# Layer 2 projections from the unnormalised residual, retention scores by row halves, and regrouped memory waits in a fused transformer kernel

## The reference, cut to what matters

```
mem_n = rmsnorm(mem, mem_norm_g)
for i in range(2):
    h = rmsnorm(x, norm_g[i])                  # x * rsqrt(mean(x*x)+eps) * g
    proj = h @ w_in                            # 1024 -> q, k, v, q_mem, z
    main = fox_attention(...) if i == 0 else retention(...)
    memo = mem_cross_attention(q_mem, mem_n, w_mem_kv[i])
    o = concat([main, memo]) * silu(z)         # 12 main heads, 4 memory heads
    x = x + o @ w_out[i]

retention, 12 heads, key width 64, value width 128:
    q, k = rotary(q), rotary(k) * 64 ** -0.5
    scores = (q @ k.T) * decay(head, lag)
    out = scores @ v                           # in chunks, with a carried state
    out = out * rsqrt(mean(out*out)+eps)
```

## Time and profile before

| | |
|---|---|
| median of 3 runs | 1745.95 us |
| profiled execution, device time | 1745.99 us |
| its span, first to last instruction | 1744.2 us |
| PE busy | 1668.8 us, 96% |
| DVE, ACT, POOL busy | 778.2, 661.2, 677.4 us |
| mean granted TensorE clock | 0.982 |
| share of PE in the chain that ended last | 85% |

### The profile page before, as it was taken

One profiled execution on the slowest core, in us unless ns is written; L12 is line 12 of the kernel. 1 busy time (PEld: TensorE's weight loads), 2 busy tenths in 40 slices (PEclk: granted clock), 3 DMA queues, 4 the chain that ended last, 5 costly groups with the idle time before them and its releaser, 6 DMA issues.

```text
span 1744.2 us, 19924 instructions
## 1 busy us (share of the span) xinstructions
PE 1668.8 (96%) x8216; PEld 1364.2 (78%) x8216; DVE 778.2 (45%) x1117; ACT 661.2 (38%) x962; POOL 677.4 (39%) x320
## 2 busy tenths in 40 slices
PE   8899999999999899999999999989989899999997
PEld 7788788788878687888887758678878688888885
DVE  6338987666664333343442645752262411111113
ACT  8433332333322342444444353235534443232322
POOL 0444324343434433333333325442402365464642
PEclk9999999999999899999999999999999899999999
DMA  6223534342435222222322222121201222222221
GB/s 246 92 104 134 176 131 154 126 144 98 151 121 172 82 85 85 97 95 96 97 92 99 75 106 85 48 84 55 70 1 49 73 97 97 97 97 97 97 85 48
DMA packets 52386, 175.99 MB, mean 101 GB/s; under 512 B 6332, under 2 KB 6972, under 8 KB 51912
## 3 DMA queue, kind: packets, MB, share of 16 engines
q1 hardware_dynamic: 52296, 174.73, 28.8%
HBM read 169.44 MB, written 2.12 MB: 98 GB/s over the span
## 4 chain that ended last, share of the span: by engine, by line
PE 85%; DVE 9%; ACT 3%; issue 1%; POOL 1%; DMA 1%; DVEq 0%; SPq 0%; ACTq 0%
PE banks L77 85%; DVE T L77 1%; DVE Sc L77 1%; DVE TM L77 1%; ACT L77 1%; POOL wl L77 1%; DVE X L77 1%; DVE HL L77 1%; ACT R L77 1%; DVE ada L77 0%; ACT T L77 0%; DVE Y L77 0%; ACT Sc L77 0%; DVE QG L77 0%; ACT wh L77 0%
## 5 line engine op out<-in xcount | busy, mean ns | idle before, releaser
L77 POOL TENSOR_TENSOR wl<-raw,wh 128x1024 fp32r<-128x1024 f32 x237 | 583.7, 2470 | 714.2 <-ACT wh L77 714.0
L77 PE MATMUL banks<-HH,wh 128*128 128x512 f32 x1040 | 418.4, 402 | 21.2 <-ACT HH L77 15.9
L77 PE MATMUL banks<-HL,wh 128*128 128x512 f32 x1040 | 411.0, 395 | 1.6 <-DVE HL L77 0.8
L77 ACT ACTIVATE wh<-raw 128x1024 fp32r<-128x1024 f32 x246 | 257.7, 1054 | 391.1 <-PE banks L77 363.5
L77 PE MATMUL banks<-HH,wl 128*128 128x512 f32 x1040 | 283.7, 393 | 0.2 <-POOL wl L77 0.2
L77 PEld LDWEIGHTS banks<-HH,wh 128*128 128x128 f32 x1040 | 198.1, 190 | 68.1 <-ACT HH L77 18.1
L77 PEld LDWEIGHTS banks<-HL,wh 128*128 128x128 f32 x1040 | 197.8, 190 | 49.6 <-DVE HL L77 5.3
L77 PEld LDWEIGHTS banks<-HH,wl 128*128 128x128 f32 x1040 | 197.6, 190 | 42.0 <-POOL wl L77 0.6
L77 PE MATMUL banks<-wh,HH 128*128 128x256 f32 x448 | 128.6, 287 | 2.0 <-ACT QX L77 2.0
L77 PE MATMUL banks<-wl,HH 128*128 128x256 f32 x448 | 127.5, 285 | 0.0
L77 PE MATMUL banks<-wh,HL 128*128 128x256 f32 x448 | 127.5, 285 | 0.0
(11 more groups left out here) (293 smaller groups left out, 2514.9 us busy)
## 6 DMA issues: line engine op xcount, KB each, us to landing
raw<-wst_dram SPq DMA_DIRECT2D x294, 512.0 KB, 3.2
CB<-sums_dram SPq DMA_DIRECT2D x12, 256.0 KB, 3.1
D<-dec_dram SPq DMA_DIRECT2D x12, 256.0 KB, 2.6
X<-xT_dram SPq DMA_DIRECT2D x4, 512.0 KB, 5.9
out_dram<-X SPq DMA_DIRECT2D x8, 256.0 KB
QS<-QX SPq DMA_DIRECT2D x24, 64.0 KB, 2.7
KSw<-KX SPq DMA_DIRECT2D x24, 64.0 KB, 2.0
MX<-memT_dram SPq DMA_DIRECT2D x2, 512.0 KB, 9.1
```

What stands on the lines that cost most here:

```text
L77: i = w[0](*w[1], **w[2])
```

## The change

1. **Layer 2 without its root mean square.** After step n of `project_out(0)`, `scaled_halves` makes HH and HL of tiles 2n and 2n+1 at once, as x times g1, and the squares are summed after that. `next_h` and the normalisation are gone. The first `unit_f` of layer 2 goes through its tiles one at a time in both banks (`by_k`), each matmul waiting for its tile only; between its two weight units `scales` makes the scale RS on PE and ACT. Queries, gates and values are multiplied by RS as banks are emptied, and COS and SIN are multiplied by RS once. These two DVE instructions stand between the second unit's gate and `mem_turn(0)`.
2. **Retention scores by row halves.** QA and QB become one tile QR; scores of both heads of a pair are matmuls of 64 rows (0 to 63, 64 to 127) into banks 2, 3 and 5, 4. All eight stand together after the values unit. The second head has its own PTodd. The norm of the first head moves into the middle of the next pair's first `unit_f`, the norm of the second head is split around the scores, and the copy of q (`keep_q`) gets a call of its own, ahead of `mem_turn(3)` in the first pair.
3. **Memory part of layer 1.** Waits for keys and values are kept per layer. The first gate stands ahead of `mem_scores(0, 0)`, and the first two `mem_values` use banks 5 and 6 in place of 0 and 1. Ten `ada` entries come in this part, and the attention pairs hold one entry to a unit.
4. In `project_out`, the squares into ACC2 come after both tiles' squares into ACC. The filter's table FO is loaded later, since PTodd lies there.

```diff
 weight_plan:
-    kv(0, 2)
-    kv(0, 3)
-    kv(1, 0)
+    for l, j in ((0, 2), (0, 3), (1, 0)):
+        kv(l, j)
+        ada(left.pop())
     pair("fox", 0, 8, (4876,))
-    kv(1, 1)
-    kv(1, 2)
+    ada(left.pop())
+    ada(left.pop())
+    for l, j in ((1, 1), (1, 2)):
+        kv(l, j)
+        ada(left.pop())
     pair("fox", 0, 8, (5132 + 1792,))
+    ada(left.pop())
+    ada(left.pop())
     kv(1, 3)
+    ada(left.pop())
...
             ada(left.pop())
-            if p < 3:
-                ada(left.pop())
 features, by_k:
+            for k in range(4):
+                kk = kts[k]
+                for nt in range(2):
+                    b, wa, wb = banks[nt], w[0][:, k, 128 * nt:128 * nt + 128], w[1][:, k, 128 * nt:128 * nt + 128]
+                    s0 = first and k == 0
+                    mm(b.ap[:, 0:n], wa, xh[:, kk, 0:n], s0, False, after=[mh, after.high[kk], *(b.free if s0 else ())])
+                    mm(b.ap[:, 0:n], wb, xh[:, kk, 0:n], False, False, after=[ml])
+                for nt in range(2):
+                    b, wa = banks[nt], w[0][:, k, 128 * nt:128 * nt + 128]
+                    e = mm(b.ap[:, 0:n], wa, xl[:, kk, 0:n], False, last and k == 3, mark=(k == 3), after=[after[kk]])
+                    b.done = e
 project_out:
-                if l == 0 and t == 7:
-                    last_square(X[:, t, :], [m])
+                if l == 0:
+                    scaled_halves(X, "g1", t, HH, HL, h1, m, [M["h read"]])
                 else:
                     add_square(X[:, t, :], T, t == 0, [m, *M["pt readers"]])
+            if l == 0:
+                for t in (2 * n, 2 * n + 1):
+                    add_square(X[:, t, :], T, t == 0, [M["x", t], *M["pt readers"]])
 layer 1, memory part:
     unit_f(HH, HL)
     m = afn(CB[:, :], CB[:, :], ACT.Ln, after=[m], bias=one)
+    for j in range(2):
+        M["z", j] = gate_in(j, [], Zt[:, j, :], RX)
     mem_scores(0, 0)
...
-    mem_values(0, 0, bank[0])
-    mem_values(0, 1, bank[1])
+    mem_values(0, 0, bank[5])
+    mem_values(0, 1, bank[6])
 layer 2, memory part:
-hs = next_h(lambda k: P("g1", k))
-layer_mem(1, hs, [M["pe"]])
+    unit_f(HH, HL, T, h1, by_k=True, beside=ret_scale)
+    for j in range(2):
+        store_q(j, QSCALE, pe_done, RX)
+    mem_scores(1, 0)
+    unit_f(HH, HL)
+    for j in range(2):
+        M["z", j] = gate_in(j, pe_done, Zt[:, j, :], RX)
+    M["cos"] = tt(COS[:, :], COS[:, :], RS[:, :], ALU.mult, after=[m_cos, M["rx"]])
+    M["sin"] = tt(SIN[:, :], SIN[:, :], RS[:, :], ALU.mult)
+    mem_turn(0)
+    mem_scores(1, 1)
+    mem_attend(1, 0)
...
 retention:
+    PLACE = {0: (2, 0, 5, 0), 1: (3, 0, 4, 0), 3: (3, 384, 4, 384), 2: (2, 0, 5, 0)}
+    def one(j, odd):
+        i, o = PLACE[j][2 * odd:2 * odd + 2]
+        rows = slice(64 * odd, 64 * odd + 64)
+        e[j, odd] = mm(bank[i].ap[:, o:o + T - 128 * j], KR[rows, 128 * j:128 * j + 128], QR[rows, 128 * j:T], j != 3,
+                       True, after=[M["q"], M["k"], *bank[i].free], mark=True)
+    for js in ((0,), (1, 3), (2,)):
+        ...
     for p in range(6):
-        unit_f(HH, HL)
+        unit_f(HH, HL, beside=(lambda: even_norm(p - 1)) if p else None)
         if p:
             ret_attend(2 * p - 1)
+            keep_q()
         else:
+            keep_q()
             mem_turn(3)
             mem_attend(1, 3)
         rotate(p)
         if p:
             ret_square(2 * p - 1)
         unit_t(HH, HL)
-        store_v([M["v read"]])
+        store_v([M["v read"]], RXC)
+        if p:
+            ret_rstd(2 * p - 1)
+        ret_scores(p)
         if p:
             ret_norm(2 * p - 1)
-        ret_scores(2 * p)
         unit_f(HH, HL)
         for j in range(2):
-            M["z", j] = gate_in(j, [M["z read"]], Zt[:, j, :])
+            M["z", j] = gate_in(j, [M["z read"]], Zt[:, j, :], RX)
         ret_attend(2 * p)
         ret_square(2 * p)
-        ret_scores(2 * p + 1)
-        ret_norm(2 * p)
+    even_norm(5)
```

169 lines of the change are left out of this document (91 added, 78 removed).

## The result

The changed kernel takes **1732.8 us** (median of 4 runs, 1731.0 to 1736.8) beside 1746.2 for the one before (1744.7 to 1747.1): a ratio of 0.9934, 95% interval 0.9919 to 0.9949. That is 13.4 us less. The forecast was 31.4 us less, 1714.5, with a range of 1703 to 1727: the sign is right, and the size lies outside the range. The profiled execution took 1731.9 us, its span is 1729.9.

What follows compares the result with a forecast made beforehand. The prediction took PE, busy 96% of the span, as the bound, so only its work and holes count. Its terms summed to -31.4 us against 1746.0: forecast 1714.5 us, range 1703 to 1727.

Steps and rivals of the forecast that it cites:

- (c): Memory part: ten ada entries delay DVE's evictions, a new hole of 2.9 us plus clock; +5.5 us, between 0 and +10.
- (a): Memory part: first gate ahead of the scores and values in banks 5 and 6 remove PE's wait and half clock; -9.3 us.
- (b): Memory part: waits kept per layer, so attends no longer wait for the other layer's keys and values; -3.9 us.
- DVE becomes the bound in the memory part: Rival: ada instructions held by POOL stop PE two or three times more; 1724 us, chance 0.14.
- (d): Attention pairs 2 and 3: one ada entry to a unit shortens the holes before key eviction Kt; -6.5 us.
- (e): Start of layer 2: without its normalisation, the stretch from output projection to first scores shrinks; -10.8 us.
- (f): Layer 2, before the first values unit: keep_q ahead, its copy made under the transposes; -3.7 us.
- (g): Layer 2: COS and SIN times RS on DVE, between gate and second PT copy, delay the attend's second half; +0.8 us.
- (h): even_norm(5): matmul of squares right behind its attend, so PE waits for one square on ACT; +0.75 us.
- (j): Retention: scores by row halves overlap in part, 0.75 us a pair, less 1.0 us for banks; -3.5 us.
- (i): Output projection: squares into ACC2 after both tiles, one hole shrinks by 1.4 us, another grows by 0.7; -0.7 us.
- (k): Retention: later rotation leaves KR in time for the scores; 0 us, between 0 and +13.

Runs made afterwards that it cites:

- gate_and_banks: The kernel before with only the first gate ahead of scores (0,0) and the first two values in banks 5 and 6, old table kept: 1740.6 us.
- four_mends: query_and_gate with an earlier weight split before scores (0,0), even_norm(5) one step later, and ACC2 squares tile by tile again: 1709.3 us.
- five_singles: four_mends with five of the ten ada entries back in the memory part, none two in a row: 1717.3 us.
- old_table: The changed kernel with the earlier weight_plan: no ada entry in the memory part, two to a unit in the first three pairs: 1716.6 us.
- padded_scores: The changed kernel with each head's queries zero padded to 128 rows again, order of scores kept: 1740.1 us.
- gate_back: old_table with the first gate back behind mem_scores(0, 0) and the scan, values still in banks 5 and 6: 1725.3 us.
- query_and_gate: The changed kernel without ada entries in the memory part, eight extra ones behind query and gate units of four pairs: 1712.4 us.
- none_behind_key: The changed kernel without ada entries in the memory part, extra ones behind query, value and gate units of the first three pairs: 1719.3 us.

## Why the prediction was wrong

The step that sank the forecast is (c), the cost of the `ada` entries in the memory part: +5.5 in the sum, +17.6 in the runs. The terms follow in their order.

**(a) -9.3, measured -3.7 by the median and -5.2 at `ident,CT`.** The step "both go" was right for Zt. What failed is "next late there is the transposes of head 0": next late were the weights. The gate's step of ACT and DVE moved the exponentials of the scores from 53.90 to 55.66, the copies of wh stand behind them on ACT, POOL's splits behind those, and PE waited 2.0 us on wl in gate_and_banks, with the clock at half for 3.4 us behind it. I had looked at the banks and at DVE, not at the splitting of weights.

**(b) -3.9, measured -5.6 on top of gate_and_banks and -6.9 in four_mends.** The mechanism was right, and so was the size of the waits: 3.9 us of them go in the first case. The 1.7 us beside them are a clock step on wl that one kernel has and the other has not, so that part is not shown to be the lists' work. In four_mends the first wait on km is 2.50 us and not 1.46, and a clock step stands behind it. (a) and (b) together are -10.8 at `ident,CT`, where I had -13.2: most of what is missing is the wait of 2.1 us on wl.

**(c) +5.5 (0 to +10), measured +17.6.** At (c) I followed one entry, the pair of `ada` instructions ahead of km, and found its wait right (2.9 forecast, 3.39 measured, 4.22 in five_singles). Then I counted it once. The same thing happened at Qt, where I wrote 0.9 us without working it out, though my own reading of the earlier trace rows said that DVE's SBUF work takes about three times as long while POOL runs, and two of the four instructions did (3.46 and 3.36 us). Measured: 3.55 us and the clock's 1.7. And the wait of 5.71 us on vm came through the weight slots, a way that stands nowhere in the forecast. The four waits less the 2.1 on wl, which old_table has too, are 12.6 us, and three clock steps at 1.7 are 5.1: together the 17.6 that lie between the two kernels at `ident,CT`, within 0.2.

The rival "DVE becomes the bound in the memory part" is, near enough, what happened. It had a chance of 0.14 and a time of 1724, so even it was too mild. Its "against", that DVE was idle half of the time, was the wrong measure: a mean over 89 us says nothing about the 5 us ahead of an eviction. The mark that I had set for being wrong, more than 8 us of idle PE in that part, was met with 14.7.

**(d) -6.5, measured -2.8.** The waits on Kt went as forecast: 0.68 us and no clock step behind it. But the first pair paid: the new waits there, PE in order of time, are 1.18 us on mod at 157.7 and 0.90 on PT at 159.7, and the stretch from 151 to 165 has DVE busy 13.15 of 14 us and a clock of 0.88:

```profile
151.00:165.00 14.00, 11.91 (x54) 9.63 (x53) 13.15 (x13) 2.22 (x3) 6.73 (x3) 0.88 0.58 204
```

That is 2.1 + 1.7 us, the difference. From 139.5 to 160 DVE has but one gap, of 0.70 us, so part of this is carried over from the memory part. But another thing came along: the accumulator has its eight entries earlier now, and its reduction (mod) stands at 156.38, in the first pair, where old_table has it at 204.09. old_table has no entry in the memory part, two to a unit in this pair, and neither wait; which of the two causes weighs more was not tried. What I missed was the boundary: a stage's debt is not settled at its end, and what follows an entry moves with it.

**(e) -10.8, measured -10.3.** The stretch is 9.5 us shorter with a group of `ada` transposes, 0.85 us (592.58 to 593.43), moved into it. The two waits were forecast as 0.5 and 0.7 us and are 0.33 and 0.56. Of all terms the largest, and the best: it was built from the length of the whole stretch and a list of what must remain in it.

**(f), (g), (h).** padded_scores separates them from (j). Its stretch from the first `km,Qt` to the first scores of retention is 74.05 us, in place of 76.71 before: -2.7, and forecast was -2.9 for (f) and (g). From there to the first `OH` it takes 2.2 us more than before, and (h) had 0.75 of that. 0.69 us of it are the wait on SQ, and another 0.66 a wait on KR that the changed kernel does not have. The remainder of 0.85 I can't place.

**(i) -0.7, measured +1.2 in its stretch.** The wait on X fell by 0.6 us (2.13 to 1.53), where I had 1.4, and that on ACC grew by 0.87 (2.78 to 3.65), where I had 0.7. That is +0.3 already, and the clock's step behind the longer wait, 3.4 us at half speed, adds 1.7. The two are more than the 1.2; the rest of the stretch was not taken apart. I had charged that price in (c) and (d), and not here.

**(j) -3.5, measured -7.0.** The two bounds held it. The base was misread: the eight take 4.13 us before and not 4.3, since a first head's four take 1.97 and not 2.16. The guess that two records of a matmul run strictly in order, so that only the last half of one meets the first of the next, gave 0.75 us a pair, and 1.0 was measured; full overlap would be 2.07. What orders them was not tried. The loss of 1.0 us on banks 2 and 5 is there in part: PE's matmuls name no wait, but the weight loads of the last blocks wait 0.30 us a pair on DVE's PTodd, within the 3.13. And 0.7 of the 7.0 are a wait on KR in padded_scores. The changed tiling has next to no price: a group of sixteen records starts 0.96 us behind SQ's start (715.48 to 716.44), and HH follows it at 719.57. The rule that changing the mode drains TensorE (the Trainium skill, TensorEngine Tiling (Array Packing), Key Properties) may hold, but no more than 0.1 us of it shows here: in padded_scores the group starts 0.86 us behind SQ's start (717.88 to 718.74).

**(k) 0, measured 0.** PE's matmuls have no wait on KR in the changed kernel's six pairs; weight loads have one, of 0.8 us. KR takes 0.69 us now (at 758.12), since POOL's hold falls elsewhere, as the text had said.

In sum, by the runs: (a) and (b) -10.8, (c) +17.6, (d) -2.8, the projection -2.6, (e) -9.5 in its stretch, (f) to (h) and (j) -7.5, (i) +1.2. That is -14.4, against -14.3 between the spans and -13.4 between the medians.

## What to carry to other kernels

Work that no one waits for still costs, when it stands in an in-order engine's queue ahead of something that is waited for, and when it holds a slot that the critical engine's next load needs. Before such work is moved into a stretch "where the engine is half idle", count the instructions between each bank's last matmul and its eviction, at the duration they have there and not at their best. And look behind a large wait before you price it: the 6.87 us on Zt hid one of 2.0 us on wl, so the edit which took it away gained less than the trace of before shows.

## What the runs showed of the hardware

- DVE's instructions with all operands in SBUF are held while POOL's split runs, whatever their own length. In gate_back POOL is idle from 50.6 to 64.28, and the same three instructions that took 3.28, 2.89 and 3.30 us in the changed kernel (shown in the first section) are these, DVE in order of time:

```profile
57.02 1.14 DVE L77 TENSOR_SCALAR Sc<-Sc,rs 128x256 f32<-128x256 f32 x4
58.08 0.69 DVE L77 TENSOR_TENSOR CB<-CT,CB 128x512 f32<-128x512 f32 x1
58.80 1.23 DVE L77 TENSOR_TENSOR_SCAN CT<-ones,CB 128x512 f32<-128x512 f32 x1
```

  That is 3.1 us in place of 9.5. km, which reads a bank, takes 0.68 us with POOL at work. `ada` is 1.27 us alone, and 3.3 to 3.5 beside POOL: some 2.2 us on top of its own time, close to one split of POOL (7.57 us for three and 4.75 for two, 2.4 to 2.5 each). The Trainium skill (SBUF — State Buffer, section SBUF: two separate sides) says that a DVE instruction in a two-port mode or with two inputs in SBUF, and a GpSimd instruction, take a shared pair of ports for the whole instruction, the other one waiting; the rows agree with a hold of one split.
- Float32 matmuls of two row halves, in separate banks, overlap in part: the same eight take 3.13 us in place of 4.13, 24% less, where full overlap would be 2.07. The 3.13 hold a wait of 0.30 us of the last weight loads.
- The granted clock fell to 0.5 for 3.4 us behind some waits and not behind others of the same length. old_table and query_and_gate run the same program up to the first `ident,CT`, and both wait on wl, 2.10 and 2.11 us. The clock stays at 1.00 in the first and is 0.5 from about 61.6 to 65.0 in the second. The wait of 3.01 us on Sc at the start of the output projection is in every kernel here. In none_behind_key the clock fell right after it (485.4 to 488.8), and in query_and_gate it did not, with the same rows ahead. What decides it was not tried, so each such step is 1.7 us that a sum of this kind can miss by, and that a comparison of two traces can show without a cause in the edit.
